# Encoder trunk on one core: first weight slot, convolution's rounding, key roots and pair loads each moved in the engines' orders

## The reference, cut to what matters

```
layer 0: h += [conv module | differential attention](rms_norm(h)) @ w_out
layer 1: h += RWKV-7 time mixing, forward and backward scans
         kk = k * k_k;  kk = kk / max(sqrt(sum(kk^2 per head of 64)), 1e-12)
both:    h += cross_attention(rms_norm(h), 256 memory tokens);  h += relu(rms_norm(h) @ up)^2 @ down
out:     rms_norm(h)
```

## Time and profile before

| what | us |
|---|---|
| median of 3 runs (range) | 1931.05 (1930.81 to 1932.45) |
| the profiled execution's own time | 1928.18 |
| its span | 1926.4 |
| TensorE matmuls busy | 1859.2 (97%) |
| VectorE, ScalarE, GpSimd busy | 1055.7, 755.4, 174.2 |

### The profile page before, as it was taken

The page is one execution under the profiler, slowest core; times in us unless marked ns, Lnnn a source line. Parts: engine busy times, 40 slices in busy tenths (PEclk is TensorE's granted clock), DMA queues, the critical chain, the costliest instruction groups (busy, mean ns, idle before and its releaser), DMA issues.

```text
span 1926.4 us, 38666 instructions
## 1 busy us (share of the span) xinstructions
PE 1859.2 (97%) x17053; PEld 1529.8 (79%) x17053; DVE 1055.7 (55%) x1405; ACT 755.4 (39%) x1006; POOL 174.2 (9%) x136
## 2 busy tenths in 40 slices
PE   6999899999999999999999999999999999999997
PEld 4898558778888888775679898899787788888886
DVE  5897665444432443447648888787664344324422
ACT  4434674334421332323844343343643353213322
POOL 1000002000000000210003211111120010000000
PEclk9999999999999999999999999999999999999999
DMA  6227223112332232443441111112352132332221
GB/s 213 84 72 233 77 99 131 66 44 91 106 110 87 88 110 90 153 137 126 153 140 50 50 50 51 50 47 69 125 197 88 33 99 87 110 103 88 94 88 44
DMA packets 165503, 189.41 MB, mean 98 GB/s; under 512 B 11801, under 2 KB 152646, under 8 KB 163674
## 3 DMA queue, kind: packets, MB, share of 16 engines
q1 hardware_dynamic: 162016, 174.44, 28.2%
q0 software_dynamic: 3088, 12.45, 1.6%
q10 hardware_dynamic: 234, 0.06, 0.0%
HBM read 161.22 MB, written 21.51 MB: 95 GB/s over the span
## 4 chain that ended last, share of the span: by engine, by line
PE 48%; DVE 5%; issue 2%; ACT 2%; DMA 0%; ACTq 0%; DVEq 0%; SPq 0%
PE ps L357 10%; PE ps L359 10%; PE ps L358 10%; PE ps L2353 7%; PE ps L2319 2%; PE ps L2366 2%; PE ps L2307 1%; PE ps L1743 1%; PE ps L2330 1%; PE ps L1313 1%; PE ps L2412 1%; PE ps L2449 1%; PE ps L1294 1%; DVE s_inverse_t L2683 1%; PE ps L2286 1%
## 5 line engine op out<-in xcount | busy, mean ns | idle before, releaser
L344 DVE TENSOR_TENSOR weights_split<-w,weights_split 128x2048 fp32r<-128x2048 f32 x116 | 265.7, 2290 | 235.3 <-ACT weights_split L326 230.5
L326 ACT ACTIVATE weights_split<-w 128x2048 fp32r<-128x2048 f32 x118 | 225.5, 1911 | 288.7 <-PE ps L359 270.2
L357 PE MATMUL ps<-x_hn_hi,weights_split 128*128 128x512 f32 x640 | 252.7, 395 | 0.0
L359 PE MATMUL ps<-x_hn_hi,weights_split 128*128 128x512 f32 x640 | 249.2, 389 | 0.0
L358 PE MATMUL ps<-x_hn_lo,weights_split 128*128 128x512 f32 x640 | 249.0, 389 | 0.0
L357 PE MATMUL ps<-f_hidden_hi,weights_split 128*128 128x512 f32 x512 | 199.3, 389 | 0.0
L359 PE MATMUL ps<-f_hidden_hi,weights_split 128*128 128x512 f32 x512 | 199.2, 389 | 0.0
L358 PE MATMUL ps<-f_hidden_lo,weights_split 128*128 128x512 f32 x512 | 199.2, 389 | 0.0
L1563 DVE SCALAR_TENSOR_TENSOR f_relu<-ps,x_squares 128x512 f32<-128x512 f32 x64 | 44.1, 691 | 191.1 <-PE ps L359 172.5
L358 PEld LDWEIGHTS ps<-x_hn_lo,weights_split 128*128 128x128 f32 x640 | 120.2, 188 | 26.2 <-issue 1.4
L357 PEld LDWEIGHTS ps<-x_hn_hi,weights_split 128*128 128x128 f32 x640 | 120.2, 188 | 26.0 <-issue 1.4
(11 more groups left out here) (365 smaller groups left out, 3513.6 us busy)
## 6 DMA issues: line engine op xcount, KB each, us to landing
w<-in_ffn_w_up_dram SPq DMA_DIRECT2D x32, 1024.0 KB, 5.4
w<-in_ffn_w_down_dram SPq DMA_DIRECT2D x32, 1024.0 KB, 4.8
w<-in_xattn_w_kv_dram SPq DMA_DIRECT2D x15, 1024.0 KB, 5.5
w<-in_ab_w_in_dram SPq DMA_DIRECT2D x10, 1024.0 KB, 5.0
w<-in_xattn_w_q_dram SPq DMA_DIRECT2D x8, 1024.0 KB, 4.9
w<-in_xattn_w_o_dram SPq DMA_DIRECT2D x8, 1024.0 KB, 4.7
w<-in_ab_w_out_dram SPq DMA_DIRECT2D x4, 1024.0 KB, 5.3
w<-in_rwkv_w_r_dram SPq DMA_DIRECT2D x4, 1024.0 KB, 6.5
```

Of the source, the lines that this page charges most:

```text
L326: act.activation(hi, raw, ACT.Copy).then_inc(k.w_hi_ready, 1)
L344: eng.tensor_tensor(lo, raw, hi.bitcast(F32), ALU.subtract).then_inc(k.w_lo_ready, 1)
L357: pe.matmul(out, lhs[0], rhs[0], start=start, stop=False)
L359: return pe.matmul(out, lhs[1], rhs[0], start=False, stop=stop)
```

## The change

1. **Start.** ACT rounds slot 0 right behind the roots, ahead of its copies of x, and copies chunks 4 to 7 (chunk 5 too). DVE copies chunks 0 to 3, makes the diagonals, and takes the rest of slot 0 ahead of its wait for the row of roots.
2. **Attention.** `A` of chunks 0 to 3 moves from steps 1, 2, 3, 4, ahead of `d`, to the ends of steps 1, 3, 5, 7.
3. **Key phase.** ACT does the roots in pairs in steps 3, 5, 7, 9: two Ln, one wait, two Exp. DVE's product comes one step later.
4. **Scan.** At `bn` of pair p only the v row of pair p+2 is loaded. The kk and r rows of pair p+2 are loaded behind `ua` and `ub` of pair p, and the k row of pair p+1 behind `qb` of pair p, for pairs 2 to 7. PE's wait in VT stays as it is.

```diff
@@ stage_in, in_act
+        ws.round(act, 0)
+        for c in range(4, C):
-        for c in (4, 6, 7):
@@ stage_in, in_dve
-        for c in (0, 1, 2, 3, 5):
-            if c == 5:
-                dve.wait_ge(s_root, 1)
-                for a in range(4):
-                    dve.tensor_scalar(diag[:, a, :], k.ident, xst[:, 8 + a:9 + a], None, ALU.mult) \
-                       .then_inc(s_diag, 1)
+        for c in range(4):
...
+        dve.wait_ge(s_root, 1)
+        for a in range(4):
+            dve.tensor_scalar(diag[:, a, :], k.ident, xst[:, 8 + a:9 + a], None, ALU.mult).then_inc(s_diag, 1)
+        ws.rest(dve, 0)
@@ Differential, order of step i
-            if 1 <= i <= 4:
-                order.append(("A", i - 1, 0))
...
             if i >= 2:
                 order.append(("t", i - 2, 0))
+            if i in (1, 3, 5, 7):
+                order.append(("A", i // 2, 0))
@@ rin_act
-                if 2 <= t < 10:
-                    b = t - 2
-                    k.wait_freed(act, num[("n", b)])
-                    k.act.link(act, act.activation(rn[:, b % 4, :], rn[:, b % 4, :], ACT.Ln))
-                    act.activation(rn[:, b % 4, :], rn[:, b % 4, :], ACT.Exp, scale=-0.5).then_inc(s_rt, 1)
+                if 3 <= t < 11 and t % 2:
+                    b = t - 3
+                    for n in (b, b + 1):
+                        k.wait_freed(act, num[("n", n)])
+                        k.act(act.activation(rn[:, n % 4, :], rn[:, n % 4, :], ACT.Ln))
+                    k.act.wait(act)
+                    for n in (b, b + 1):
+                        act.activation(rn[:, n % 4, :], rn[:, n % 4, :], ACT.Exp, scale=-0.5).then_inc(s_rt, 1)
@@ rin_dve
-                if 3 <= t < 11:
-                    b = t - 3
+                if 4 <= t < 12:
+                    b = t - 4
@@ load_pair, and scan_sp
-def load_pair(k, sp, p):
-    for a, src in enumerate((k.d_r, k.d_kk, k.d_k, k.d_v)):
+def load_pair(k, sp, p, rows=range(4)):
+    for a in rows:
+        src = (k.d_r, k.d_kk, k.d_k, k.d_v)[a]
...
-                        load_pair(k, sp, p + 2)
+                        load_pair(k, sp, p + 2, [3])
+                elif kind in ("ua", "ub", "qb"):
+                    q = p + 1 if kind == "qb" else p + 2
+                    if 2 <= q < C:
+                        taken(sp, kind.upper(), p)
+                        load_pair(k, sp, q, [{"ua": 1, "ub": 0, "qb": 2}[kind]])
```

## The result

| | before | after |
|---|---|---|
| median, us (range) | 1931.75 (1930.81 to 1936.07) | 1943.99 (1942.89 to 1945.46) |
| ratio, 95% interval | | 1.0059, 1.0043 to 1.0075 |
| profiled execution, us | 1928.18 | 1944.15 |
| mean granted clock of PE over the span | 0.994 | 0.990 |

The changed kernel is 12.2 us slower (11.4 by the ratio). The forecast was 5.2 slower, 1936.2; the measured time lies above its range, which ended at 1942. In the table of the experiments two slow executions, 2344 us of the kernel "burst moved" and 3175 us of before beside it, are left out.

A forecast was written before the change was run, and what follows sets the result against it. PE, busy 97% of the span, was taken as the bound, so edits pay only in its idle time. The terms -1.1 - 3.7 - 4.8 + 14.0 + 3.3 - 2.5 gave +5.2, 1936.2 us against the median; range 1927.5 to 1942.

The forecast's parts named there:

- Part 1: Start: PE's first product comes at 22.0 instead of 23.04, 1.1 us gained; nil if slot 0 lands 1 us later.
- Part 2: Attention: PE's early gaps go, the fourth A waits behind ACT's root; net 3.7 us gained, between 2.5 and 7.2.
- Part 3: Key phase: paired roots save 8 of 16 table loads and v0 starts earlier; 4.8 us gained (3.3 to 5.8).
- Part 4: Scan, pair loads: waits at VT cost 14.0 us and the clock 3.3, shorter gaps return 2.5.
- VT's waits: Scan: VT waits for the late k row, landing in 2.7 us, in six periods; 14.0 us lost (10.4 to 17.6).
- The clock: Scan: three of the six new gaps drop PE's clock, about 1.1 us each; 3.3 us lost (0 to 6.6).
- The relief: Scan: a burst one row smaller shortens two long PE gaps, read as held-up instruction fetches; 2.5 us gained (0 to 5.7).
- SP's waits and the k row's place: Scan: SP's new waits at `ua`, `ub` and `qb` have nothing late behind them; no cost.
- Rival 1: Scan: k row lands in 2.1 us, clock holds at all six gaps, fetch gaps go wholly; 1926.2 us, chance 0.2.
- Rival 2: Scan: every new gap drops the clock and the fetches gain nothing; 1942.0 us, chance 0.15.
- Rival 3: Scan: gaps without releaser aren't fetches behind row loads, so the spread returns nothing; 1938.7 us, chance 0.2.
- Rival 4: Attention or key phase: Part 2 or Part 3 doesn't do what it says, about 3.7 us more; 1939.9 us, chance 0.1.

The follow-up runs named there:

- burst moved: Parts 1 to 3, with all four rows of pair p+2 issued together behind `gb` instead of `bn`: 1945.2 us, 1.0053 of the kernel before.
- parts 1 to 3: The changed kernel with all four rows of a pair loaded at `bn`, as before: 1922.2 us, 0.9947 of the kernel before.
- A earlier: A at steps 1, 3, 4, 5 instead of 1, 3, 5, 7: on parts 1 to 3 1919.8 us, 0.9926; with the rows apart too 1916.8 us, 0.9907.
- part 3 alone: The kernel before with only the key roots done in pairs: 1926.1 us, 0.9976 of the kernel before.
- part 4 alone: The kernel before with only the pair loads of the changed kernel: 1954.3 us, 1.0110 of the kernel before.
- rows really apart: Pair p+2's rows behind `bn`, `tb`, `qb` and `gb`: on parts 1 to 3 1918.2 us, 0.9914; on the kernel before 1927.7 us, 0.9980.

## Why the prediction was wrong

**What bounds it.** Right: nothing was gained or lost but by PE's gaps and the clock behind them.

**Part 1**, forecast 1.1. PE starts 1.7 us earlier in the changed kernel (21.36), and 1.2 earlier in the trace of parts 1 to 3 (21.85), where the start is the same: the forecast was about right. A clock fall behind the start, at 46 to 50 us in the trace of before, is also gone, worth 1.7 more; the run with parts 1 to 3 has one again in its first 60 us (3.4 us lost between 43 and 50), so this isn't part 1's.

**Part 2**, forecast 3.7. PE's way from 150.20 to 275.89 before is from 146.81 to 268.71 after, 3.8 shorter. The number was right and the way to it was not. As written, the terms (7.2, 3.1 of new waits, 0.4 of an old gap that goes) give 4.5, and not 3.7. The new wait is where it was put, behind ACT's root, but PE stands only 0.80 us there, not 3.1, and pays 1.7 more by the fall at 233, which the forecast hadn't; in the trace of parts 1 to 3, without that fall, two more gaps of 0.85 and 0.54 us stand in its place. Timeline of the changed kernel, ACT and DVE:

```profile
229.49 0.58 ACT L1087 ACTIVATE difference_t<-ps 128x512 f32<-128x512 f32 x1
229.97 0.62 ACT L405 ACTIVATE x_src_hi<-cat 128x512 fp32r<-128x512 f32 x1
...
230.69 0.69 DVE L410 TENSOR_TENSOR x_src_lo<-cat,x_src_hi 128x512 fp32r<-128x512 f32 x1 [4.80 <-ACT x_src_hi L405]
```

DVE waits 4.80 us for the fourth A, and the scores behind it reach PE 0.80 late. With that A ahead of the root (the runs with A earlier) another 2.4 us come, 6.4 less than before in all, near the bound of 7.2.

**Part 3**, forecast 4.8, for v0's gap 1.2. The gap is 1.41. From the product behind PE's gap of 0.33 us near the start of the phase to v0 it took 47.6 us (894.65 to 942.24) where it took 50.8 (900.20 to 950.95), 3.2 less, and from v0 to the first VT 1.6 less, the clock fall of the earlier trace rows that is gone: 4.8, as forecast. (The steps named there add up to 946.6 for v0, 1.1 short of the 947.7 that the forecast went by; part 3 alone has 947.90.) The fall behind v0 isn't one that comes and goes: it stands in all four traces without part 3 and in none of the ten with it. The loads at the roots are 8 in place of 16, and that the loads between Ln and Exp cost time is borne out. By the rule of the Trainium skill, "ScalarE: Activation LUTs", on table sets, pairing would have given nothing. The trace and the run of part 3 alone speak against it here. A fall of 1.7 us at 820 to 824, which before doesn't have, takes back what the one at 46 gave; such falls come and go.

These three come to 9.6 in the forecast, 10.3 in the trace and 10.2 by the ratio.

**Part 4.** Four terms, with a cost of 14.8 against 21.5 measured:

- *VT's waits*, forecast 14.0 with a landing of 2.7. Measured 15.8, landing 2.9 with the row loaded alone. Mis-sized by 1.8: the waits don't follow `qb` to VT as unevenly as in the trace of before, from 1.86 to 2.7; all are near 2.6.
- *The clock*, forecast 3.3, three of six gaps at 1.1 each. **This term failed.** By the mean clock of all executions (0.9900 against 0.9932, of 1930 us) it is 6.2 us (with 0.9918, the lowest mean that the kernel before has on any chip, 3.5); by part 4 alone (0.9892 against 0.9931, the same chip) 7.5; by the two profiled scans 8.5, one of its falls behind a gap without releaser. The number of falls was nearly right, four of six. The size wasn't: 1.1 was read from one stretch of 3.5 us that ended before the clock was back. Followed to its end the same fall of before loses 1.7, and one of the new ones lost 3.4. I priced a step that happens six times by one window of one gap. (Of the six waits in the trace of part 4 alone, 2.27 to 2.86 us, again four fell, for 1.7 each.)
- *The relief*, forecast 2.5 gained. **This term failed as well.** The mechanism was right, fetches held up by row loads, and the size was not. No gain stands clear of the noise: gaps without releaser 12.1 us in sum in the changed kernel, 12.3 without part 4. I had scaled each gap by a quarter less traffic. But three rows in a burst stretched it as four did; only rows really apart stretched it less.
- *SP's waits and the k row's place*: right, nothing is queued behind them that was late.

15.8 + 6.2 + 0 = 22.0, against 21.3 and 21.7 measured. Of the 7 us that the forecast missed, 1.8 lie in the waits, some 3 in the clock (2.9 by 6.2, 4.2 by 7.5) and 2.5 in the relief.

**The rivals.** Rival 1 (not slower) is refuted: the row landed in 2.9 us, the clock fell behind four waits, and the gaps stayed. Rival 2 (all six gaps drop the clock, no relief: 1942.0) came nearest; its premise was wrong, four of six, and its price of 1.1 too, and the two errors nearly cancel. Rival 3 (no relief, since the gaps have nothing to do with row loads) had the right relief for the wrong reason: that row loads stretch these gaps is now shown, and their places and the packets ahead of their ends show that PE waits there for instructions. The rule in the Trainium skill, "Runtime: NRT & Kernel Launch", section "Instruction fetch mechanics", is that such a fetch is mostly hidden. By their number that fits: in the scan of before 83 packets came and 7 gaps of 0.3 us or more. It doesn't say how long the others last, 0.34 and 0.69 us at the two places without row loads and 2.26 and 2.86 with them. Rival 4 (part 2 or 3 does nothing) is refuted by the 10.3 us of the first three parts.

**The base.** The sum was set against a profiled execution 2.9 us under its median. Its scan took 388.7 us, that of parts 1 to 3 in the profiled execution 394.3, with the same instructions in it, most of the difference clock (6.8 us lost, against 1.7) behind gaps without releaser. A trace is one draw: 29 executions of the kernel before on one chip took 1925.5 to 1938.1 us.

## What to carry to other kernels

Before moving a load, look at what the semaphore behind it counts: where one wait covers four rows, the latest row sets the start of the consumer of all, and moving it near costs its whole landing each time. On an engine that is busy 97%, price a wait together with the clock behind it, and by whole falls: here 1.7 or 3.4 us more behind most waits of 2.5 to 2.9 us and, in the key phase and the scan, behind every gap of over 3.1. Spreading traffic helped here only where the pieces ended up apart; three issues in a row were still one burst. And in a program as long as this one, look for gaps without a releaser at equal steps of the instruction count: they are waits for instructions, and here their length went with what was in flight when the packet was due.

## What was not expected of the hardware

- Waits of 2.50, 2.59, 2.66 and 2.67 us were followed by half the clock, those of 2.56 and 2.82 weren't, and the fall behind 2.66 lasted over 6 us where the others lasted 3 to 4. Nothing that I read in these traces tells them apart; this stays open. Over all the profiled scans, each fall lost 1.7 or 3.4 us by the sum of one less the clock, nothing in between.
- PE's gaps without releaser stand at multiples of 126 matmuls, one packet of the instruction queue. Where they come at all they keep their instruction over all kernels, and at L2408 (L2398 before) they range from 0.34 us with no rows in flight to 3.43 with them.
- A row of 256 KB alone landed in 2.9 us; three issued in a row behind two stores took 3.9 to 4.5 each (medians).
